# Sums of squares added up in one row set on GpSimd, and multiplied by ones as rounded-fp32 products

## The reference, cut to what matters

```
def rmsnorm(x, g):
    xf = x.astype(jnp.float32)
    y = xf * lax.rsqrt(jnp.mean(xf * xf, axis=-1, keepdims=True) + EPS)
    return (y * g.astype(jnp.float32)).astype(x.dtype)

def layer_fwd(x, ...):
    x = x + 0.5 * swiglu(rmsnorm(x, g_ffn1), f1_in, f1_out)
    z = rmsnorm(x, g_mix) @ w_in
    ...
    x = x + concat(pool, attention, retention) @ w_out
    x = x + 0.5 * swiglu(rmsnorm(x, g_ffn2), f2_in, f2_out)
```

## Time and profile before

| | us |
|---|---|
| median of 3 runs | 1324.78 |
| lowest and highest of them | 1323.68 and 1326.86 |
| the profiled execution | 1329.16 |
| its span, from the first to the last instruction | 1327.5 |

### The profile page before, as it was taken

One profiled execution on the slowest core, in us unless ns is written; L12 is line 12 of the kernel. 1 busy time (PEld: TensorE's weight loads), 2 busy tenths in 40 slices (PEclk: granted clock), 3 DMA queues, 4 the chain that ended last, 5 costly groups with the idle time before them and its releaser, 6 DMA issues.

```text
span 1327.5 us, 27075 instructions
## 1 busy us (share of the span) xinstructions
PE 1308.2 (99%) x10985; PEld 1258.4 (95%) x10985; DVE 764.2 (58%) x787; ACT 652.6 (49%) x736; POOL 236.9 (18%) x375
## 2 busy tenths in 40 slices
PE   8999999999999999999999999999999999999998
PEld 6999999998868999999999999999897699999998
DVE  5555555676656655564555555565866665555433
ACT  6555543435435555553365555333445555555433
POOL 3000000357551100000101000012856220000010
PEclk9999999999989999999999999999999999999999
DMA  7555544558696444444445554446597944444442
GB/s 235 183 181 181 162 138 155 193 176 223 207 326 205 131 154 158 141 136 149 151 152 188 184 168 148 147 146 212 159 260 244 330 146 156 136 151 158 142 147 67
DMA packets 209821, 233.15 MB, mean 176 GB/s; under 512 B 14974, under 2 KB 202632, under 8 KB 209748
## 3 DMA queue, kind: packets, MB, share of 16 engines
q1 hardware_dynamic: 200508, 205.16, 48.2%
q0 software_dynamic: 9120, 26.94, 6.4%
q10 hardware_dynamic: 120, 0.03, 0.0%
HBM read 226.90 MB, written 5.32 MB: 175 GB/s over the span
## 4 chain that ended last, share of the span: by engine, by line
PE 94%; DMA 2%; DVE 2%; issue 1%; ACT 1%; SPq 1%; DVEq 0%; ACTq 0%
PE ps L1421 24%; PE ps L1419 24%; PE ps L1420 24%; PE ps L1535 4%; PE ps L1537 4%; PE ps L1536 4%; PE ps L1685 2%; PE ps L1726 2%; DMA kbuf<-in_cache_k 1%; PE ps L1867 1%; DMA w_raw<-in_ffn_w_in 1%; PE ps L1869 1%; PE ps L1868 1%; PE ps L1702 1%; PE ps L1493 1%
## 5 line engine op out<-in xcount | busy, mean ns | idle before, releaser
L685 ACT ACTIVATE w_hi<-w_raw 128x2048 fp32r<-128x2048 f32 x167 | 319.6, 1914 | 529.8 <-PE ps L1421 423.6
L999 DVE TENSOR_TENSOR w_lo<-w_raw,w_hi 128x2048 fp32r<-128x2048 f32 x159 | 364.8, 2294 | 198.4 <-ACT w_hi L685 193.8
L1419 PE MATMUL ps<-h_hi,w_hi 128*128 128x320 f32 x768 | 238.0, 310 | 3.0 <-DVE w_lo L999 2.3
L1421 PE MATMUL ps<-h_hi,w_lo 128*128 128x320 f32 x768 | 237.3, 309 | 0.0
L1420 PE MATMUL ps<-h_lo,w_hi 128*128 128x320 f32 x768 | 237.3, 309 | 0.0
L1419 PE MATMUL ps<-g_hi,w_hi 128*128 128x320 f32 x704 | 217.8, 309 | 0.0
L1421 PE MATMUL ps<-g_hi,w_lo 128*128 128x320 f32 x704 | 217.4, 309 | 0.0
L1420 PE MATMUL ps<-g_lo,w_hi 128*128 128x320 f32 x704 | 217.4, 309 | 0.0
L1420 PE MATMUL ps<-act_lo,w_hi 128*128 128x320 f32 x704 | 216.5, 308 | 0.0
L1421 PE MATMUL ps<-act_hi,w_lo 128*128 128x320 f32 x704 | 216.5, 308 | 0.0
L1419 PE MATMUL ps<-act_hi,w_hi 128*128 128x320 f32 x704 | 216.5, 308 | 0.0
(11 more groups left out here) (303 smaller groups left out, 1748.8 us busy)
## 6 DMA issues: line engine op xcount, KB each, us to landing
w_raw<-in_ffn_w_in SPq DMA_DIRECT2D x87, 1024.0 KB, 5.1
w_raw<-in_ffn_w_out SPq DMA_DIRECT2D x32, 896.0 KB, 4.5
w_raw<-in_w_in SPq DMA_DIRECT2D x22, 1024.0 KB, 5.3
kbuf<-in_cache_k SPq DMA_DIRECT2D x96, 192.0 KB, 3.3
w_raw<-in_ffn_w_out SPq DMA_DIRECT2D x16, 1024.0 KB, 4.9
kbuf<-in_cache_v SPq DMA_DIRECT2D x44, 192.0 KB, 5.7
w_raw<-in_w_out SPq DMA_DIRECT2D x8, 1024.0 KB, 9.6
kbuf<-in_cache_k POOLq DMA_DIRECT2D x32, 192.0 KB, 2.8
```

The lines of the kernel that those rows point to most:

```text
L685: act.activation(w_hi[:, slot, :], w_raw[:, slot, :], ACT.Copy).then_inc(hi_done, 1)
L999: dve.tensor_tensor(w_lo[:, slot, :], w_raw[:, slot, :], w_hi[:, slot, :].bitcast(F32), ALU.subtract).then_inc(split_done, 1)
L1419: pe.matmul(out, w_hi[:, slot, w], hi[:, k, :], start=(k == 0), stop=False)
L1421: ins = pe.matmul(out, w_lo[:, slot, w], hi[:, k, :], start=False, stop=(k == k_all - 1))
```

## The change

`ssq` gets the type fp32r. GpSimd keeps a running sum of 320 elements in `rstd` instead of one of 640 in `ssq`: the two halves of each slot of squares are added to it one after the other. At the fourth step the last addition is made twice, once with its output written to `ssq[:, 0]` in fp32r, which rounds it, and once in fp32 into `rstd`; then the rounded part is subtracted from the full one and the rest is written, rounded, to `ssq[:, 1]`. `sum_squares` multiplies the two parts by ones read as fp32r. At the last norm `token_sums` gets the running sum as one part where it had two halves.

```
-        ssq = sb("ssq", [P, 2, TOK])
+        ssq = sb("ssq", [P, 2, TOK], F32R)
...
                     if j == 0:
                         wait_apart(pool, sq_done, q + (j + 1))
-                        pool.tensor_copy(ssq[:], s).then_inc(ssq_done, 1)
+                        pool.tensor_tensor(rstd[:], s[:, 0, :], s[:, 1, :], ALU.add).then_inc(ssq_done, 1)
                     else:
                         pool.drain()
                         pool.wait_ge(sq_done, q + (j + 1))
-                        pool.tensor_tensor(ssq[:], ssq[:], s, ALU.add).then_inc(ssq_done, 1)
+                        pool.tensor_tensor(rstd[:], rstd[:], s[:, 0, :], ALU.add)
+                        pool.drain()
+                        if j < 3:
+                            pool.tensor_tensor(rstd[:], rstd[:], s[:, 1, :], ALU.add).then_inc(ssq_done, 1)
+                        else:
+                            pool.tensor_tensor(ssq[:, 0, :], rstd[:], s[:, 1, :], ALU.add)
+                            pool.tensor_tensor(rstd[:], rstd[:], s[:, 1, :], ALU.add)
+                            pool.drain()
+                            pool.tensor_tensor(ssq[:, 1, :], rstd[:], ssq[:, 0, :].bitcast(F32), ALU.subtract).then_inc(ssq_done, 1)
...
             def sum_squares(n):
                 pe.wait_ge(ssq_done, n * 4)
-                pe.matmul(ps[:, 4, 0:TOK], ones[:], ssq[:, 0, :], start=True, stop=False)
-                pe.matmul(ps[:, 4, 0:TOK], ones[:], ssq[:, 1, :], start=False, stop=True).then_inc(stat_done, 1)
+                pe.matmul(ps[:, 4, 0:TOK], ones[:].bitcast(F32R), ssq[:, 0, :], start=True, stop=False)
+                pe.matmul(ps[:, 4, 0:TOK], ones[:].bitcast(F32R), ssq[:, 1, :], start=False, stop=True).then_inc(stat_done, 1)
...
             def token_sums(u, squares, first, last):
                 m = P if u < 2 else SMP
-                for a in range(2):
-                    ins = pe.matmul(ps[0:m, 2 + u % 2, u // 2:u // 2 + 1], squares[:, a, u * P:u * P + m], ones[:, 0:1],
-                                    start=first and a == 0, stop=last and a == 1)
+                for a, part in enumerate(squares):
+                    ins = pe.matmul(ps[0:m, 2 + u % 2, u // 2:u // 2 + 1], part[:, u * P:u * P + m], ones[:, 0:1],
+                                    start=first and a == 0, stop=last and a == len(squares) - 1)
                 return ins
+
+            early, late = [rstd], [sq_slot[1][:, a, :] for a in range(2)]
...
-                token_sums(u, ssq, True, False)
+                token_sums(u, early, True, False)
...
-                ins = token_sums(u, sq_slot[1], False, True)
+                ins = token_sums(u, late, False, True)
```

More of the change, by code:

```diff
@@ L1930, in _ @@
             pe.wait_ge(std_tok, 1)
-            token_sums(2, ssq, True, False)
-            token_sums(2, sq_slot[1], False, True).then_inc(tok_done, 1)
+            token_sums(2, early, True, False)
+            token_sums(2, late, False, True).then_inc(tok_done, 1)
             to_tokens(2, range(6, KT)).then_inc(y_tr, 1)
```

## The result

| | before | after |
|---|---|---|
| median, us | 1326.86 (15 runs) | 1330.65 (15 runs) |
| lowest and highest, us | 1321.81 and 1332.19 | 1328.30 and 1335.26 |
| span of the profiled execution, us | 1327.5 | 1331.0 |

The ratio is 1.0032, with a 95% interval of 1.0020 to 1.0044. That is 4.2 us longer, 2.7 to 5.8; the two medians are 3.8 us apart. (The median of before is now over 15 runs; the 1324.78 ahead was over the first three.)

What follows compares the result with a forecast made beforehand. TensorE, busy 1308.2 of 1327.5 us, was taken to bound the kernel. Five places, each 1.71 us of wait less 0.79 gained, give 4.6; less 0.4 at the end, 4.2 longer: 1324.78 to 1329.0, range 1325.0 to 1332.0.

Steps and rivals of the forecast that it cites:

- What TensorE gets back: At five `sum_squares` places the two products take 0.29 us instead of 1.08: 0.79 us gained each, 3.95 in all.
- What the end gets back: At the kernel's end, four weight loads for `ssq` products instead of eight: 0.4 us less.
- What GpSimd needs: GpSimd's last step: four 320-element instructions, 0.75 us per add, 0.8 for the subtraction, 0.7 after a wait, drains 0.15.
- What is in the way: VectorE's L999 interrupts GpSimd's chain after L528; TensorE gets the sum 6.62 us after last squaring starts (T), waiting 1.71.
- The sum: Over the whole kernel: five places each 0.92 us longer, 4.6, less 0.4 at the end: 4.2 us longer.
- The clock: Over the profiled execution, TensorE was read as at full clock in every slice.
- The rest of the change: First three GpSimd steps, some 0.2 us longer each, and later DMAs before the mixer cost nothing; 0.5 us slack left.
- that the engines don't block each other: Rival: at the places GpSimd and VectorE run side by side, TensorE never waits; 4.35 us gained, time 1320.4; chance 0.13.
- Short operations: Rival: GpSimd's 320-element operations take 0.6 us each, TensorE waits 1.0; about 0.5 us longer, time 1325.3; chance 0.15.
- That GpSimd keeps its turn: Rival: GpSimd goes on past L528's end, L999 ends at T+5.6 to T+6.6; 3 to 4 us longer; in forecast's chance.
- Long operations: Rival: GpSimd's operations take 0.9 us each, TensorE waits 2.3; 7 us longer, time 1332; chance 0.06.
- That the order matters little: At the places, GpSimd's 3.0 us and L999's 2.15 together fill the time; the order of both engines changes little.

Runs made afterwards that it cites:

- products in fp32: The changed kernel with both products by ones given fp32 operands again; ratio to before 1.0068, FFN stretch (last squaring to last squaring over a feed-forward part) 235.28 us.
- half of the subtraction: The changed kernel with VectorE's subtraction at the five places over 1024 of 2048 columns, the other low weights left stale; ratio to before 1.0006, FFN stretch 233.45 us.
- last step on VectorE: The changed kernel with the last step's four 320-element operations on VectorE, ahead of its subtraction, instead of GpSimd; ratio to before 0.9968, FFN stretch 232.71 us.
- the reordered kernel: The changed kernel with products by ones after 15 second-chunk matmuls, and third chunk's hi and lo parts ahead of root and reciprocal; ratio to before 0.9991.
- the version with the products later: The changed kernel with products by ones after 15 matmuls of the second chunk, ScalarE's and VectorE's order kept; ratio to before 1.0043, FFN stretch 234.46 us.

## Why the prediction was right, point by point

It said 1329.0 from a median of 1324.78, 4.2 us longer; measured were 4.2 (2.7 to 5.8), with 1330.65, within the range. That 1330.65 lies 1.7 above 1329.0 is due to the base: the median of before over 15 runs is 2.1 above that over three. The mechanism was as forecast at all five places.

- **What TensorE gets back**: 0.79 a place forecast. Putting the fp32 products back cost 0.78. The Trainium skill, FP8 and Floating Point Precision, "TensorE Precision Notes", counts four passes for true fp32, which would have made it an estimated 0.87; the trace doesn't bear this size out, and it was rightly not used.
- **What the end gets back**: 0.4 forecast, 0.44 in the weight loads.
- **What GpSimd needs**: this term was under-sized. An operation of 320 elements took 0.86 to 0.89 us where I had 0.75 and 0.8, and 0.72 after a wait where I had 0.7. The chain ended at T+6.78 instead of T+6.54, and TensorE's weight load was 1.92 late instead of 1.71. Of this 0.05 came back, since two products and two matmuls behind the wait took 0.53 (258.84 to 259.37) where I had four steps, 0.58. So a place cost 1.09, not 0.92. The 0.69 us estimated from the rate in the Trainium skill, GPSIMD Engine Reference, "3.1 Elementwise — side-by-side cycle accounting", is near the 0.72 after a wait and 0.17 to 0.20 short of an operation that didn't wait.
- **What is in the way**: right in its order. L1007 took its turn in the middle of the chain and ended 2.14 us after L528's end (254.92 to 257.06; forecast 2.15), as the L999 at 294.68 had done.
- **The sum**: with the measured sizes it would be 5 x 1.09 - 0.44 = 5.0 us. The traces show 4.0 from the first place's T to the end (1074.98 before, 1078.99 after). What is missing is in one stretch that has the first layer's mixer: 185.45 us before and 185.46 after, though it holds a place too. That the total came out at 4.2 is partly luck: the sum with this term right is 0.8 higher, and the mixer differs by more than that between executions. The interval of 2.7 to 5.8 holds both sums.
- **The clock**: the prediction read full clock in every slice. The row has an 8 in the twelfth slice, so less than 0.9 was granted there. That slice lies in the first mixer; what goes on there is told below. No place of the change is in it, so no term was hurt.
- **The rest of the change**: the first three steps cost nothing that the traces show. ScalarE's squarings are as far apart as before in the feed-forward part, and no wait of TensorE for GpSimd stands beside the five. GpSimd's later DMAs left 0.49 us before the mixer's first tiles where 3.58 had been; the forecast was 0.5.
- **The rivals**: that the engines don't block each other fell with L529's 2.91 us, and with 0.89 and 1.86 when VectorE's instruction was moved or halved. Short operations fell with 0.88. That GpSimd keeps its turn fell with L1007, which went between L528 and L529. Long operations, 0.9 each, were nearer than their chance of 0.06 says: those that didn't wait took 0.86 to 0.89. But the two that had waited took 0.72 and 0.75, so that the wait was 1.92 and not 2.3. That the order matters little was shown by holding VectorE back: 234.51 for 234.50.

## What to carry to other kernels

When a step is moved onto GpSimd or made longer there, lay it beside VectorE's timeline and add up both engines' instructions up to the moment at which the consumer needs them: GpSimd's that read SBUF and VectorE's with two inputs there, the kinds that met here. Each instruction end in a chain is a place where the other engine's long instruction gets in. (Whether a drain is one too isn't shown: no meeting here fell in one.) A few short two-input operations on a small tile were cheaper on VectorE (0.49 us each against 0.88) in a gap that it had anyway. And size small effects by a stretch that repeats to a few hundredths of a microsecond within one execution, at the same granted clock, not by the whole time.

## What was not expected of the hardware

- In the nine traces, one of each kernel, the stretch with the first layer's mixer took 180.1 to 188.0 us and that with the second's 179.2 to 183.4, where the feed-forward stretches of one execution agree to 0.03. With what the edit itself changes at the one place in each stretch taken off, 181.0 to 186.1 and 180.0 to 181.6 are left. A good part of the first goes with TensorE's granted clock. In five of the nine executions (before, changed, products in fp32, half of the subtraction, last step on VectorE) it was 0.50, the 1.2 GHz level, for some 10 us on end in that mixer; these are the five that took 184.4 or more. Of the other four, with 183.5 or less, two had 0.58 over 4 us and two stayed at 1.00. In the kernel before TensorE had stood idle for 1.44 us just ahead of it, up to 381.80. But in the reordered kernel it stood idle for 1.16 us at the same matmuls, and the clock stayed at 1.00. Before (upper) and reordered (lower), from the view by stretches:

```profile
384.00:388.00 4.00, 4.00 (x36) 2.70 (x35) 1.50 (x3) 0.44 (x1) 0.00 (x0) 0.50 1.05 364
```
```profile
384.00:388.00 4.00, 3.79 (x47) 2.46 (x44) 2.58 (x8) 1.76 (x5) 0.00 (x0) 1.00 1.04 364
```

  (The numbers are busy us and instructions of PE, PEld, DVE, ACT and POOL, then granted clock, DMA share and GB/s.) The whole time goes with the clock too: of 29 executions of the kernel before, the six with a mean granted clock of 0.999 took 1324.4 us on average, the five with 0.994 took 1328.9. What decides whether the clock falls, and the rest of the mixer's spread, stay open.
- Ahead of the feed-forward parts, going from the square root back to a copy cost ScalarE a table load of 1.28 us. Ahead of the first mixer the copy of the changed kernel started at 259.86, while the root that had begun at 259.43 (0.53 long) was ending, with no load between. With hi and lo parts ahead of the root, ScalarE had two loads at a feed-forward place (at 441.79 and 443.63) where the version with the products later had three (at 438.03, 443.94 and 447.17); the FFN stretches are 232.90 and 234.46 us. How much of this is the load and how much VectorE's new order wasn't separated.
